# Two hybrid parts that start on unnormed x and scale four slabs afterwards

## The reference, cut to what matters

```
h = rms_norm(x, mix_norm[l])                  # x * rsqrt(mean(x*x)) * norm weight
z = h @ w_in[l]                               # 1024 x 3592
hq, hf, hi, hg, fq, fk, fv, ff = split(z)     # 7 x 512 columns and 8 forget gates
logf_h = logaddexp(log(lb), log1p(-lb) + log_sigmoid(hf));  k_h = (1 - lb) * sigmoid(-hf)
q_h = silu(hq);  o_h = rms_norm(scan(q_h, k_h, hi, logf_h)) * silu(hg)
o_f = forgetting_attention(fq, fk, fv, log_sigmoid(ff + bias))
x = x + concat(o_h, o_f) @ w_out[l]
```

## Time and profile before

| | us |
|---|---|
| median of 3 runs | 2659.59 |
| fastest, slowest run | 2656.63, 2660.51 |
| span of the profiled execution | 2655.6 |
| TensorE busy | 2598.7 |
| VectorE busy | 1661.0 |
| ScalarE busy | 1354.8 |
| POOL busy | 149.1 |

### The profile page before, as it was taken

The page is one execution under the profiler, slowest core; times in us unless marked ns, Lnnn a source line. Parts: engine busy times, 40 slices in busy tenths (PEclk is TensorE's granted clock), DMA queues, the critical chain, the costliest instruction groups (busy, mean ns, idle before and its releaser), DMA issues.

```text
span 2655.6 us, 48868 instructions
## 1 busy us (share of the span) xinstructions
PE 2598.7 (98%) x21606; PEld 2526.7 (95%) x21606; DVE 1661.0 (63%) x1970; ACT 1354.8 (51%) x1671; POOL 149.1 (6%) x227
## 2 busy tenths in 40 slices
PE   8999999999999999999999999999999999999998
PEld 8989999899998999999999999989999999999998
DVE  5667555475476755676656656765656657764764
ACT  5745545554446544674545445555445446554543
POOL 4400000100000000430000000000000000000000
PEclk9999999999999999999999999999999999999999
DMA  7515564456544565452665765445666755344763
GB/s 218 166 33 161 195 234 137 153 176 222 191 147 145 177 222 175 144 150 99 195 240 176 192 226 173 143 144 143 191 192 190 192 193 165 118 133 132 197 198 129
DMA packets 429971, 451.97 MB, mean 170 GB/s; under 512 B 13346, under 2 KB 395024, under 8 KB 427584
## 3 DMA queue, kind: packets, MB, share of 16 engines
q1 hardware_dynamic: 417952, 416.12, 50.3%
q0 software_dynamic: 7312, 32.35, 3.5%
q10 hardware_dynamic: 4496, 0.39, 0.1%
HBM read 441.21 MB, written 7.60 MB: 169 GB/s over the span
## 4 chain that ended last, share of the span: by engine, by line
PE 86%; DVE 6%; ACT 5%; issue 1%; POOL 1%; DMA 1%; ACTq 0%; SPq 0%; DVEq 0%; POOLq 0%
PE ps L603 85%; ACT wH L1504 2%; DVE wL L2142 2%; ACT hidden_parts L1564 1%; DMA ring<-in_gdn_w_in 0%; POOL arena L503 0%; DVE arena L2677 0%; PE ps L1030 0%; DVE hT L2398 0%; ACT L1531 0%; PE ps L1248 0%; DVE arena L2406 0%; POOL arena L505 0%; DMA arena<-leaf_out 0%; ACT sq L1759 0%
## 5 line engine op out<-in xcount | busy, mean ns | idle before, releaser
L2142 DVE TENSOR_TENSOR wL<-ring,wH 128x2048 fp32r<-128x2048 f32 x392 | 898.3, 2292 | 753.8 <-ACT wH L1504 753.4
L1504 ACT ACTIVATE wH<-ring 128x2048 fp32r<-128x2048 f32 x392 | 753.4, 1922 | 1004.6 <-PE ps L603 1002.4
L603 PE MATMUL ps<-hidden_parts,wH 128*128 128x256 f32 x6656 | 989.5, 277 | 3.8 <-ACT hidden_parts L1564 3.0
L603 PEld LDWEIGHTS ps<-hidden_parts,wH 128*128 128x128 f32 x6656 | 900.6, 188 | 5.8 <-issue 3.8
L603 PE MATMUL ps<-hidden_parts,wL 128*128 128x256 f32 x3328 | 693.3, 276 | 1.4 <-DVE wL L2142 1.3
L603 PEld LDWEIGHTS ps<-hidden_parts,wL 128*128 128x128 f32 x3328 | 522.0, 188 | 1.8 <-DVE wL L2142 1.8
L603 PE MATMUL ps<-hH,wH 128*128 128x256 f32 x2624 | 366.8, 281 | 5.9 <-DVE hH L2159 3.2
L603 PE MATMUL ps<-hH,wL 128*128 128x256 f32 x2624 | 358.1, 278 | 2.3 <-DVE wL L2142 2.3
L603 PE MATMUL ps<-hL,wH 128*128 128x256 f32 x2624 | 345.7, 278 | 0.0
L603 PEld LDWEIGHTS ps<-hH,wH 128*128 128x128 f32 x2624 | 328.4, 189 | 15.2 <-issue 12.8
L603 PEld LDWEIGHTS ps<-hH,wL 128*128 128x128 f32 x2624 | 326.2, 188 | 3.0 <-DVE wL L2142 2.9
(11 more groups left out here) (305 smaller groups left out, 1967.1 us busy)
## 6 DMA issues: line engine op xcount, KB each, us to landing
ring<-in_mlp_w SPq DMA_DIRECT2D x128, 1024.0 KB, 5.4
ring<-in_ffn_w_gate SPq DMA_DIRECT2D x88, 512.0 KB, 4.0
ring<-in_ffn_w_up SPq DMA_DIRECT2D x88, 512.0 KB, 5.3
ring<-in_ffn_w_down SPq DMA_DIRECT2D x44, 1024.0 KB, 5.0
ring<-in_gdn_w_in SPq DMA_DIRECT2D x32, 1024.0 KB, 5.9
ring<-in_w_in SPq DMA_DIRECT2D x28, 1024.0 KB, 5.4
hidden_parts<-mem_parts POOLq DMA_DIRECT2D x14, 1024.0 KB, 7.8
ring<-in_mlstm_w_in SPq DMA_DIRECT2D x12, 1024.0 KB, 5.3
```

Source lines behind the costliest of these rows:

```text
L603: return pe.matmul(o, l, r, start=start, stop=stop, **k)
L1504: f(wH[:, n % PARTS, :], ring[:, n % RING, :], ACT.Copy).then_inc(sem("high_split"), 1)
L2142: tt(wL[:, n % PARTS, :], ring[:, n % RING, :], wH[:, n % PARTS, :].bitcast(F32), ALU.subtract)\
```

## The change

Both hybrid parts begin like the mlp parts. ScalarE (`late_start`) writes x times norm weight as `start_x[0]` and squares x; VectorE (`late_low`) makes `start_x[1]` and sums the squares; TensorE multiplies slabs 0 to 3 and the forget gates with these halves. VectorE scales the four banks by rs into `qk` (`scaled_out`), and makes the normed x and its low half behind the first slabs (`normed`, `normed_low`) for slabs 4 and later. The forget gates' weights are split by VectorE into two fp32r halves and multiplied in 24 products. `start_x` lies where `gate` and part of `v_tok` lie, so POOL waits for slab 3 before it clears these.

```diff
+        start_x = (hidH[:, 24:32, :], hidH[:, 16:24, :])
+        fox_w = [flat_parts[:, at:at + DC * 8].rearrange("p (c n) -> p c n", c=DC) for at in (15424, 15488)]
...
                     W.chain(pool.memset(qk[64:128, 12:16, :], 0.0))
+                    pool.wait_ge(sem("products_done"), group("w_in_2", i, HYBRID_ORDER[3]))
...
                 last.then_inc(sem("products_done"), 1)
+                if behind_one:
+                    behind_one()
...
             def hybrid(l):                                            # TensorE
-                norm_sum(behind=6, filler=filled_before[("hybrid", l)], at=(0, 0, 0, 0, 10))
-                first_products("w_in_2", l, HYBRID_ORDER[0:2], DC, columns)
+                fill(filled_before[("hybrid", l)], 0, 2 * MEM_PIECES)
+                first_products("w_in_2", l, HYBRID_ORDER[0:2], DC, columns, src=start_x, behind_one=summed_norm)
...
-                        pe.wait_ge(sem("gates_in"), GATE_LOADS)
-                        for k in range(DC):
-                            last = mm(ps[0:8, 0, 0:T], gw[:, 3 + l, k, 0:8], hT[:, k, :], k == 0, k == DC - 1)
+                        pe.wait_ge(sem("gate_split"), W.next("gate_split"))
+                        last = three(ps[0:8, 0, 0:T], [lambda k: fox_w[0][:, k, :], lambda k: fox_w[1][:, k, :]],
+                                     [lambda k: start_x[0][:, k, :], lambda k: start_x[1][:, k, :]], DC)
...
                     if n >= 4:
-                        pe.wait_ge(sem("evac"), W.next("evac"))
+                        pe.wait_ge(sem("scaled_out"), W.next("scaled_out"))
+                    if n == 4:
+                        pe.wait_ge(sem("normH_ready"), W.next("normH_ready", 4))
+                        pe.wait_ge(sem("normL_ready"), W.next("normL_ready", 4))
...
+            def late_start(name, layer, j, gain, k0, filler):         # ScalarE
+                for c in range(4):
+                    act.wait_ge(sem("x_ready"), W.next("x_ready"))
+                    for k in (2 * c, 2 * c + 1):
+                        ins = f(start_x[0][:, k, :], xT[:, k, :], ACT.Copy, scale=column(gain, k0 + k))
+                    ins.then_inc(sem("hH_ready"), 1)
+                    f(sq[:, 2 * c:2 * c + 2, :], xT[:, 2 * c:2 * c + 2, :], ACT.Square).then_inc(sem("xsq_ready"), 1)
+                empty_filler(filler)
+                ln_exp()
+                split(slab_no[(name, layer, j)] + PARTS)
+                act.wait_ge(sem("ss_ready"), W.next("ss_ready"))
+                rsqrt(ps[:, 2, 0:T], rs[:, :], D, "rs_ready")
...
             def hybrid(l):                                            # ScalarE
-                x_norm("w_in_2", l, HYBRID_ORDER[0], filler=filled_before[("hybrid", l)])
-                channels("w_in_2", l, 1, 4, chunks(qk, 4))
-                act.wait_ge(sem("evac"), W.next("evac", 2))
+                late_start("w_in_2", l, HYBRID_ORDER[0], "mix_norm_2", l * DC, filled_before[("hybrid", l)])
+                for n in range(2):
+                    ready("w_in_2", l, HYBRID_ORDER[n])
+                act.wait_ge(sem("scaled_out"), W.next("scaled_out", 2))
...
                 f(glog, glog, ACT.Ln, bias=1.0).then_inc(sem("glog_ready"), 1)
+                normed_high()
...
             def hybrid(l):                                            # VectorE
-                x_norm("mix_norm_2", l * DC, "w_in_2", l, HYBRID_ORDER[0])
+                late_low("mix_norm_2", l * DC, start_x, "w_in_2", l, HYBRID_ORDER[0])
+                dve.wait_ge(sem("gates_in"), GATE_LOADS)
+                W.chain(dve.tensor_copy(fox_w[0], gw[:, 3 + l, :, 0:8]))
+                tt(fox_w[1], gw[:, 3 + l, :, 0:8], fox_w[0].bitcast(F32), ALU.subtract).then_inc(sem("gate_split"), 1)
...
+                def scaled_out(n):
+                    s = HYBRID_ORDER[n]
+                    dve.wait_ge(sem("products_done"), group("w_in_2", l, s))
+                    c = 2 * s if s < 2 else 4 + 2 * (s - 2)
+                    tt(qk[:, c:c + 2, :], two(ps[:, 4 + n, :]), rs_twice(), ALU.mult).then_inc(sem("scaled_out"), 1)
+
+                refill("w_in_2", l, HYBRID_ORDER[0])
+                dve.wait_ge(sem("rs_ready"), W.next("rs_ready"))
+                scaled_out(0)
+                scaled_out(1)
+                normed("mix_norm_2", l * DC)
                 refill("w_in_2", l, 3)
                 dve.wait_ge(sem("gates_done"), W.next("gates_done"))
-                ts(r(1), ps[0:8, 0, 0:T], gbias[:, 2 + l:3 + l], None, ALU.add).then_inc(sem("fz_ready"), 1)
+                W.chain(tt(r(1), ps[0:8, 0, 0:T], rs[0:8, :], ALU.mult))
+                ts(r(1), r(1), gbias[:, 2 + l:3 + l], None, ALU.add).then_inc(sem("fz_ready"), 1)
+                normed_low()
                 dve.wait_ge(sem("glog_ready"), W.next("glog_ready"))
...
                 negative_cum(r(5)).then_inc(sem("rows_ready"), 1)
+                scaled_out(2)
                 refill("w_in_2", l, 0)
+                scaled_out(3)
```

More of the change, by code:

```diff
@@ L154 @@
           "vec_in", "vec_turned", "masks_ready", "leaf_", "inverse_in",
-          "kv_", "memH_ready", "mem_normed", "act_ready", "hiddenH_ready", "hidden_ready", "o_ready", "prob_ready", "post_squared", "post_folded")
+          "kv_", "memH_ready", "mem_normed", "act_ready", "hiddenH_ready", "hidden_ready", "o_ready", "prob_ready", "post_squared", "post_folded",
+          "o_taken", "rows_ready", "log_ready")
 VECTOR_SETUP = {"lambda_sums": 1, "lb_diff": 2, "lambda_ready": 3, "lb_ready": 4, "params_ready": 5}
@@ L633, in bank_of, with first_products @@
                 return 4 + j % 4
-            def first_products(name, layer, js, c, at, src=(hH, hL), together=True):
+            def first_products(name, layer, js, c, at, src=(hH, hL), together=True, behind_one=None):
                 n = [slab_no[(name, layer, j)] for j in js]
@@ L1335, in hybrid @@
                     if n == 2:
-                        pe.wait_ge(sem("gates_in"), GATE_LOADS)
-                        for k in range(DC):
-                            last = mm(ps[0:8, 0, 0:T], gw[:, 3 + l, k, 0:8], hT[:, k, :], k == 0, k == DC - 1)
+                        pe.wait_ge(sem("gate_split"), W.next("gate_split"))
+                        last = three(ps[0:8, 0, 0:T], [lambda k: fox_w[0][:, k, :], lambda k: fox_w[1][:, k, :]],
+                                     [lambda k: start_x[0][:, k, :], lambda k: start_x[1][:, k, :]], DC)
                         last.then_inc(sem("gates_done"), 1)
                     if n >= 4:
-                        pe.wait_ge(sem("evac"), W.next("evac"))
-                    (to_tokens if s in (4, 5) else to_channels)("w_in_2", l, s, bank_of(n))
+                        pe.wait_ge(sem("scaled_out"), W.next("scaled_out"))
+                    if n == 4:
+                        pe.wait_ge(sem("normH_ready"), W.next("normH_ready", 4))
+                        pe.wait_ge(sem("normL_ready"), W.next("normL_ready", 4))
+                    (to_tokens if s in (4, 5) else to_channels)("w_in_2", l, s, bank_of(n),
+                                                                src=start_x if n < 4 else (hH, hL))
                 to_channels("w_in_2", l, 8, 1)
@@ L1554, in x_norm, with normed_high @@
                 empty_filler(filler)
+            def late_start(name, layer, j, gain, k0, filler):
[10 more added lines that the diff above has]
+                rsqrt(ps[:, 2, 0:T], rs[:, :], D, "rs_ready")
+            def normed_high():
+                for c in range(4):
+                    act.wait_ge(sem("h_ready"), W.next("h_ready", 2))
+                    f(hH[:, 2 * c:2 * c + 2, :], hT[:, 2 * c:2 * c + 2, :], ACT.Copy).then_inc(sem("normH_ready"), 1)
             def late_norm(name, layer, gain, k0, x_parts, between, filler=None):
@@ L1996, in hybrid @@
                 f(qk[:, 4:8, :], qk[:, 4:8, :], ACT.Sigmoid, scale=-1.0).then_inc(sem("hk_ready"), 1)
-                channels("w_in_2", l, 0, 6, chunks(qk, 0), func=ACT.Silu)
+                for s in range(2):
+                    ready("w_in_2", l, s)
+                    act.wait_ge(sem("scaled_out"), W.next("scaled_out"))
+                    v = qk[:, 2 * s:2 * s + 2, :]
+                    f(v, v, ACT.Silu)
                 channels("w_in_2", l, 3, 4, chunks(gate, 0), func=ACT.Silu)
@@ L2036, in hybrid @@
                         attention_slab(SLAB_ENDS[n - 1])
-                W.next("evac", 12)
                 square_pair(0, two(ps[:, 0, :]), "o_ready")
@@ L2175, in x_norm, with late_low @@
                     split(slab_no[(name, layer, j)] + PARTS)
-            def late_low(gain, k0, x_parts, name, layer):
+            def late_low(gain, k0, x_parts, name, layer, j=0):
                 for c in range(4):
@@ L2183, in late_low, with normed, normed_low @@
                     ins.then_inc(sem("hL_ready"), 1)
-                split(slab_no[(name, layer, 0)] + PARTS)
+                split(slab_no[(name, layer, j)] + PARTS)
```

(11 more changed lines are left out.)

## The result

| | before | after |
|---|---|---|
| median of 4 runs each, us | 2660.05 | 2674.28 |
| fastest, slowest run | 2656.63, 2660.54 | 2672.2, 2678.68 |
| span of the profiled execution | 2655.6 | 2672.8 |

What follows compares the result with a forecast made beforehand. TensorE, busy 98%, was taken to bound the kernel. Part 0 +2.8, part 1 +8.2 and clock +3.4 gave +14.4 on the 2655.6 span, 2670.0; with 4.0 from span to median, 2674 us, range 2662 to 2681.

Steps and rivals of the forecast that it cites:

- wait for high 1: Start of each part: TensorE waits for ScalarE's high half of w_in slab 1, 3.9 and 8.2 us.
- wait for low 4: 16 products into slab 4: TensorE waits for VectorE's low half of that slab, 2.0 and 4.3 us.
- wait for low 5: In slab 5: TensorE waits for VectorE's low half of that slab, 1.0 and 2.7 us.
- clock, both starts: TensorE's clock falls once behind each part's start wait, 1.7 us a fall, +3.4 us; bounds 0 and 6.8.
- POOL's memsets: Three memsets of 0.95 us, now beside VectorE's chain, cost 0; bounds 0 and 2.9 us per part.
- part 0 in all, a fall in it: Hybrid part 0: +2.8 us from its start, removed work and waits, plus a clock fall of 1.7.
- part 1 in all, a fall in it: Hybrid part 1: +8.2 us from its start, removed work and waits, plus a clock fall of 1.7.
- The start: ScalarE's queue ahead of slab 1's high half makes TensorE begin slab 0 later, +0.4 and +2.0 us.
- VectorE's chain: VectorE's gapless work from slab 2's low half to slab 4's, 18.2 us in part 0, 20.5 in part 1.
- What left TensorE: Norm sums, blank products and fp32 gates (3.55 us) go; 24 gate products cost 2.72; first to third slab -0.6 per part.
- The first rival: Faster: slab 1's high half is there before x's halves and VectorE's chain is hidden; -10.4 us, 2649; chance 0.06.
- The third rival: Slower still: each wait brings a clock fall and POOL's memsets hold VectorE; +19.7 us, 2679; chance 0.13.

Runs made afterwards that it cites:

- x_blank: The changed kernel with blank float32 products ahead of slab 0, 8 in part 0 and 17 in part 1, inside the start waits: 2672.63 us, ratio 1.0041.
- x_pool: The changed kernel with POOL's three last memsets waiting for slab 6 in place of slab 3: 2674.79 us, ratio 1.0054.
- x_table: The changed kernel with ScalarE's table load moved ahead of its wait for x: 2673.04 us, ratio 1.0044.
- x_start: The changed kernel with only its start mended: table load first, slab 1's high half before squares, part 1 beginning on slab 0 alone: 2660.91 us, ratio 1.0005.
- x_gates: The kernel before with only the forget gates changed, to 24 fp32r products in place of 8 float32 ones: 2660.3 us, ratio 0.9997.
- x_best: x_start's edit plus ScalarE's and VectorE's halves of later slabs moved earlier, POOL waiting for slab 7, `pair` cleared later: 2648.24 us, ratio 0.9958.
- x_order: The changed kernel with the high and low halves of slabs 4 and 5 made earlier in ScalarE's and VectorE's queues: 2674.59 us, ratio 1.0055.

## Why the prediction was right, step by step

| step | predicted | after showed |
|---|---|---|
| wait for high 1, part 0 and 1 | 3.9 and 8.2 | 3.96 and 8.24 |
| wait for low 4, part 0 and 1 | 2.0 and 4.3 | 1.56 and 6.27 |
| wait for low 5, part 0 and 1 | 1.0 and 2.7 | 0.56 and 1.11 |
| clock, both starts | 3.4 | 3.2 (x_blank) |
| POOL's memsets | 0 | 2.3 (x_pool) |
| part 0 in all, a fall in it | 4.5 | 4.4 |
| part 1 in all, a fall in it | 9.9 | 11.6 |

**The start** was read from the order of a queue. ScalarE's work between x and the high half of slab 1 was priced 5.3 for copies and squares, 1.28 and 1.93; in after it runs from 2208.79 to 2217.39, 8.60 us against 8.5. x_table took 1.4 us of it out by moving one instruction, x_start all of it.

**VectorE's chain** from the start of low 2 to the end of low 4 was counted as 18.2 and 20.5 us. It took 17.95 in part 0 (1645.40 to 1663.35) and 22.50 in part 1 (2229.72 to 2252.22). The 2.0 us too much are the second group of tensor_scalar, 3.47 instead of 1.14; x_pool's chain is without it, and its wait of 3.94 is near the 4.3. This is the term of the chain that was mis-sized: "I take 0", from a row in which a memset ran beside a low half. Part 0 of after shows that pair again and it is still free (a low half of 2.28 us at 1661.07 with memsets at 1661.16 and 1662.18). The row was of another form of instruction, and did not bound this one. The Trainium skill (SBUF — State Buffer, "Who interferes with whom") parts the two: a two-input VectorE instruction does not contend with a GpSimd instruction that only writes, while one in a two-port mode, which tensor_scalar can enter, does, and one of the two engines is blocked. The trace agrees on both, with 2.28 and with 3.47 us; the bound by the rule, 1.9 for up to two memsets, was low because all three fell on the group.

**The clock.** One fall per start was right in number, and in price on average (1.2 to 2.3 us each, see x_blank). A third came behind the wait for low 4 in part 1: granted clock 0.55 over 3.2 us, 1.4 us of product time lost. It came nearly free, as the argument about absorption had it: VectorE needed 8.2 us from low 4 to low 5 in either case, and the wait for low 5 shrank from the predicted 2.7 to 1.11. The Trainium skill (TensorE: Matmul & The Clock Gate, "Part 1: The HAM clock gate") has the low level as the default that activity releases; x_blank agrees, since work of no use in the wait kept the clock at 1.00 behind it. That does not make every fall certain, as the prediction had it for two: behind the wait of 1.56 us in part 0 the clock was 1.00 (1663.3 to 1665.0).

**What left TensorE** was right in size: the gates are 2.77 us in x_gates for 3.55, and with the start mended the saving shows.

**The errors cancelled in part.** The forecast's sum was +14.4. Part 1 took 1.7 more (low 4 +2.0 by POOL, low 5 -1.6, the third fall +1.4), part 0 0.1 less. The span was 2.8 us above the forecast's 2670.0, while the median was only 1.5 above the span, where I had taken 4.0 from before: that the median fits within 0.3 is luck of that size. The 4.0 was no property of the kernel. In every run whose span is listed, the time is 1.7 to 1.9 us above the run's own span; the rest of the 4.0, over 2 us, means that the profiled execution of before was a fast one. The two spans are therefore 17.2 us apart where the medians are 14.2. The waits confirm the reasoning, not the last digit.

**The first rival** was wrong for this kernel and right for x_best: 2649 by its sum, 2648.24 measured. It named the one point that decides, whether the first product waits for the high half of slab 1, and it put the chain of VectorE as the second thing that has to go; x_start shows that the first alone gives back the loss and no more. It priced the chain at 10 us; x_start and x_best are 12.7 apart.

**The third rival** (2679) was right in half. POOL held VectorE, by 2.3 us where it took 1.9, and one more fall came, behind low 4 of part 1; the waits for low 4 and low 5 in part 0 brought none (1.00 behind both).

**Left open.** Why the clock stayed low longer in x_table after a shorter wait isn't settled, nor why a fall behind the same wait of 3.96 us cost 1.2 us in one execution and 2.3 in another. Nor is which of x_best's later edits (low 6, low 7, the memset of `pair`) is needed: they ran together only.

## What to carry to other kernels

Here, taking work from the engine that bounds the kernel paid only once the queues of the helpers were laid out anew. So list, per helper, everything that now stands between the data and the first operand, and put the halves that the bounding engine needs next ahead of squares, table loads and evacuations. Check each reordering on all helpers at once, in the part with the most extra work. A row bounds a contention only for its own form of instruction.

## What was unexpected of the hardware

- Four tensor_scalar of 128x256 take 1.14 us, and 3.44 to 3.47 beside three memsets of 0.95 to 0.98 us on POOL (2.84 in x_order, where they began later under the memsets); the group ended 0.1 to 0.4 us behind the third memset each time. The memsets lose under 0.03 us each. VectorE pays for all.
- The wait's length does not order the cost of the clock: slab 0 to gate of part 1 was 12.88 us after a wait of 8.24 and 13.82 after one of 6.82; without a low clock it is 11.21. Behind the same wait of 3.96 us in part 0 it was 12.81 to 13.90 in four executions.
